# Issuing two experts' down blocks without waiting for the first two row gathers (one-core decoder layer)

## What is computed

```python
h2 = rms_norm(x, norm2_g) * (1 + scale2) + shift2
# hier_moe(h2, ...): the best of 4 groups, the 2 best of its 8 experts per token,
# tokens sorted by expert, then for each block of rows of one expert e:
xb = h_pad[toks]
a = xb @ w_exp_gate[e]          # (1024 x 512)
u = xb @ w_exp_up[e]            # (1024 x 512)
y = ((silu(a) * u) @ w_exp_down[e]) * wts   # (512 x 1024)
x = x + gate2 * y
```

## Time and profile before

| | us |
|---|---|
| median of 3 runs | 1310.64 |
| lowest, highest | 1309.82, 1310.77 |
| the profiled execution | 1311.63 |
| its span, first to last instruction | 1309.8 |

### The profile page before, as it was taken

How to read it: one execution, slowest core, us unless ns; L and a number is a source line. 1 busy time by engine, 2 the same in 40 slices (tenths; PEclk the granted TensorE clock), 3 DMA queues, 4 the chain that set the end, 5 groups by cost and what they waited for, 6 DMA issues and landing times.

```text
span 1309.8 us, 20856 instructions
## 1 busy us (share of the span) xinstructions
PE 1184.5 (90%) x8041; PEld 745.9 (57%) x8041; DVE 497.2 (38%) x1075; ACT 235.0 (18%) x536; POOL 235.1 (18%) x295
## 2 busy tenths in 40 slices
PE   4999998999999999999999998999987788787896
PEld 2344443475767777688888456656544444444463
DVE  3398966521324243454554456322211111111112
ACT  4122235322323232211001222000000000000000
POOL 2432344201102023340000101111111111111001
PEclk9899999999999999999999997999999999999989
DMA  9997999982654635312624627999999999999994
GB/s 355 372 278 269 361 372 385 378 330 65 248 175 142 172 94 134 98 22 57 176 84 175 257 64 209 408 414 419 410 417 419 416 418 418 416 416 416 415 413 152
DMA packets 117961, 368.17 MB, mean 281 GB/s; under 512 B 12556, under 2 KB 58525, under 8 KB 98406
## 3 DMA queue, kind: packets, MB, share of 16 engines
q1 hardware_dynamic: 93072, 304.50, 59.9%
q0 software_dynamic: 21328, 55.24, 13.7%
q10 hardware_dynamic: 3462, 7.07, 1.7%
HBM read 354.61 MB, written 22.36 MB: 288 GB/s over the span
## 4 chain that ended last, share of the span: by engine, by line
PE 63%; DMA 24%; SPq 7%; DVE 3%; issue 2%; ACT 1%; ACTq 0%; DVEq 0%; POOLq 0%
PE ps L1911 60%; DMA hx<-in_w_exp_gate 6%; DMA ring<-in_w_exp_gate 6%; SPq L549 4%; DMA ring<-in_w_exp_up 3%; DMA hx<-in_w_exp_up 3%; DMA ring<-in_w_in 3%; PE ps L1922 3%; SPq L554 2%; DMA ring<-in_cache_v 1%; DMA h_rows<-ring 1%; DVE work L1531 1%; DVE work L1866 0%; DMA work<-h_rows,idx 0%; DVE work L1641 0%
## 5 line engine op out<-in xcount | busy, mean ns | idle before, releaser
L1911 PE MATMUL ps<-ring,work 128*64 128x256 f32 (+4 forms) x2064 | 295.2, 437 | 42.1 <-DMA ring<-in_w_exp_up 17.5
L1911 PE MATMUL ps<-ring,hx 128*32 128x256 f32 (+3 forms) x1552 | 272.4, 444 | 7.4 <-ACT hx L834 4.2
L1911 PEld LDWEIGHTS ps<-ring,work 128*64 128x64 f32 (+2 forms) x2064 | 156.4, 139 | 162.8 <-issue 84.0
L1911 PEld LDWEIGHTS ps<-ring,hx 128*32 128x32 f32 (+1 forms) x1552 | 158.2, 147 | 104.1 <-issue 80.7
L1911 PE MATMUL ps<-hx,ring 128*128 128x272 f32 x704 | 163.8, 393 | 0.6 <-DVE work L1531 0.6
L1911 PE MATMUL ps<-work 128*32 128x256 f32 (+12 forms) x1186 | 135.8, 400 | 21.6 <-DVE work L1223 9.8
L1911 PEld LDWEIGHTS ps<-hx,ring 128*128 128x128 f32 x704 | 133.0, 190 | 28.7 <-DVE work L1531 1.1
L1911 PE MATMUL ps<-hx,work 128*64 128x256 f32 (+2 forms) x784 | 114.4, 414 | 22.6 <-DMA hx<-in_w_exp_up 11.4
L755 POOL DMA_INDIRECT out<-work x32 | 50.5, 1579 | 329.6 <-DVE work L1876 329.6
L1864 DVE TENSOR_TENSOR work<-work,ps 128x256 f32<-128x256 f32 x32 | 13.5, 421 | 250.6 <-ACT work L1171 250.6
L1911 PEld LDWEIGHTS ps<-hx,work 128*64 128x64 f32 (+2 forms) x784 | 66.9, 144 | 70.3 <-issue 26.4
(11 more groups left out here) (337 smaller groups left out, 949.2 us busy)
## 6 DMA issues: line engine op xcount, KB each, us to landing
ring<-in_w_exp_down SPq DMA_DIRECT2D x44, 1024.0 KB, 39.1
ring<-in_w_exp_gate SPq DMA_DIRECT2D x21, 2048.0 KB, 41.5
ring<-in_w_exp_up SPq DMA_DIRECT2D x21, 2048.0 KB, 40.9
ring<-in_w_ada SPq DMA_DIRECT2D x12, 2048.0 KB, 21.9
hx<-in_w_exp_up SPq DMA_DIRECT2D x11, 2048.0 KB, 40.7
hx<-in_w_exp_gate SPq DMA_DIRECT2D x11, 2048.0 KB, 41.6
work<-in_w_exp_down SPq DMA_DIRECT2D x20, 1024.0 KB, 39.7
ring<-in_cache_v SPq DMA_DIRECT2D x64, 256.0 KB, 10.0
```

The lines of the kernel that those rows point to most:

```text
L1911: return pe.matmul(out, lhsT, rhs, start=start, stop=stop, **k)
```

## The change

Two waits are taken out of SyncE's stream. The down blocks of experts 1 and 2 are then issued when the last logits are done and the last normed rows are stored.

```diff
             sp.wait_ge(s("lg_ps"), 5)
             sp.wait_ge(s("h2_out0"), 16 * 3)
             sp.wait_ge(s("h2_out1"), 16 * 2)
-            for p in range(2):
-                sp.wait_ge(s(f"xs_in{p}"), 16)
             down_load(1, expert_row(1))
             sp.wait_ge(s("x1_out"), 16 * PT)
             down_load(2, expert_row(2))
```

## The result

| | before | after |
|---|---|---|
| median of 5 runs, us | 1310.64 | 1316.95 |
| lowest, highest | 1309.73, 1310.98 | 1315.04, 1318.7 |
| the profiled execution | 1311.63 | 1316.95 |
| its span | 1309.8 | 1315.2 |

The ratio is 1.0048 with a 95% interval of 1.0037 to 1.0060: slower by 6.3 us. The forecast was 1311.4 us, no difference, with a range up to 1314.5. The sum leaned to the slow side by 0.8 us, the text called that no difference, and a rival had the slower outcome; none had the size.

What follows compares the result with a forecast made beforehand. DMA engines were taken to set the end. A gain of 4.2 us less a gather delay of 5.0 gave −0.8 us: 1312.4 us from the profiled execution, 1311.4 against the median, range 1307.9 to 1314.5.

Steps and rivals of the forecast that it cites:

- The sum: DMA time up to expert 3's gate load: gain of 4.2 us less d, −0.8 us with d = 5.0.
- the residual rows' wait: Wait of expert 2's down half: rows landed at 807.95 us, before the last store, so it costs nothing.
- credit: Gain from issuing the four down halves 7.5 us sooner, if the first gather is not delayed: 4.2 us.
- d: Delay of the first gather and so of TensorE's whole expert stage: 5.0 us, between 0 and 8.2.
- Rival 1: First gather hardly delayed, VectorE having slowed the third: d 1 or less, gain 3.2 to 4.2 us; chance 0.12.
- rival 3: Another wait, such as the residual rows, keeps the down halves' issue in place: 1310.6 us; chance 0.02.
- Rival 2: First gather meets a full queue: d 6.8 to 8.2, gate perhaps at the lower clock, about 1314 us; chance 0.26.
- the forecast's own band: Delay of the first gather between 1.6 and 6.8 us, with nearly no difference in time; chance 0.60.
- the sign of 821.6: First gather landing after 821.6 us would show that it met a full queue (Rival 2).
- ±1.7 us: Allowance for expert 0's gate at TensorE's lower or full clock: at most 1.7 us more, 1.8 less; costed at nothing.
- the third gather: Gather issued at 818.07 us beside the down blocks, landing after 8.2 us; taken as the first gather's nearest row.
- The rule of round robin alone: DMA engines alternate between queues by packet, so sharing alone delays the first gather: d = 3.4, gain 0.8 us.

Runs made afterwards that it cites:

- run 4: The changed kernel with VectorE idle from the index until the first gather has landed; 1314.86 us, ratio 1.0032.
- Run 2: The changed kernel, but only expert 1's two down halves go out early, expert 2's wait for both gathers; 1314.79 us, ratio 1.0038.
- run 1: The kernel before, but the down halves wait for the first gather only, not the second; 1310.98 us, ratio 1.0001.
- run 6: The changed kernel with 14, 6 or 8 extra matmuls of constants in TensorE's wait ahead of the first gather; 1317.69, 1312.96 and 1312.42 us.

## Why the prediction was wrong

**Right.** The DMA engines set the end; the halves go out at 810.4 (predicted 810.5); the residual rows' wait costs nothing; the first gather is what is delayed; the engines run dry between 824 and 832 us, and dip again before 845 (predicted near 840); the sum has the form "a credit less TensorE's lateness". With the measured x of 8.2 in place of d it gives −4.0 us, and by the bytes 4.4 were lost. Rival 1 was refuted by run 4, rival 3 by the first row of SyncE's issues. Rival 2 comes nearest, by its slower outcome and its slow gate, but not by its d: that was 6.5 and 6.2 us in the two profiles, inside the forecast's own band of 1.6 to 6.8, and the landing at 821.3 us stays under the sign of 821.6. Its 1314 us were too low. The ±1.7 us that the text kept for the clock never went into its range: 1314.5 is d near 8 alone.

**The step that failed: TensorE's lateness, taken as d = 5.0 us for the gather and nothing for the clock.** It was 8.2 us (x), and 6.8 in the second profile.

*The delay d.* Taken as 5.0 us from the third gather (8.2 us to landing), it was 6.5 and 6.2: 10.1 and 9.8 us to landing, 9.3 to 11.1 in the other runs beside 4 MB. The nearer row was the median of the later gathers, 10.3 us, which the text set aside for rival 2, because no long backlog stood ahead of the gather. Run 2 shows that 2 MB in flight are enough. The text also split the third gather's delay wrongly, into 3.4 us of sharing and 1.3 of a later start: q0's first packet came 4.6 us after that issue, where the first gather's came after 1.9, so that the later start is 2.7 us. In the changed kernel it is 3.3. The rule of round robin alone (Trainium skill, DMA: Bandwidth & Descriptors, Queues, rings and completion order), which gave 3.4 us, is further off still: it says how the queues share, and not when a gather's first packet comes or when the last engine is through.

*"Clock ... I cost it at nothing".* The row that prices it was there: a gate of 5.2 us with an up of 3.45 behind it, and the text's own bound of 1.7 us. In the profile the gate took 6.7 us, 1.5 more than before; in the second one 5.6, 0.3 more. That is no simple consequence of the longer wait, which grew from 1.9 to 9.5 us: behind a wait of 9.3 us the gate took 5.1 (run 4), and behind one of 2.4 us 6.6 (run 1). What decides when the clock comes back within the gate is not shown. The same gate takes 3.7 us when matmuls fill the wait (run 6).

**The sum.** 0.8 us were predicted and 5.6 came (y): 1.5 more by the gather, 1.5 by the gate, 0.2 by a later landing of the store, 0.4 by which the bytes lost exceed the formula, and 1.2 that no byte count shows. Over the runs with an x over 1 the credit, x less y, is 2.0 to 4.3 and not a firm 4.2. The formula treats the 16 engines as one. TensorE waits for the last of them at each load, and that the credit differs between runs fits this, but was not isolated. The medians are 6.3 and 7.1 us slower, more than these profiles show: the profile before stands 1.0 us above its median, and the second profile of the changed kernel 2.7 below its own.

## What to carry to other kernels

A transfer that is issued early into idle DMA engines was worth nothing here, because a small gather on the path had to share the engines with it: price the gather from its loaded landings, not from an idle or half-idle one. A delay ahead of TensorE's first matmuls of a stage can be paid twice, once as time and once as clock: the gate behind it took 6.7 us in one profile and 5.1 to 6.0 in four others, where 5.2 was the time before. So put what the stage takes at the lower clock into the range. Where the DMA engines set the end, ask after each move what they will do next; here they finished sooner and then waited for TensorE.

## What the runs showed of the hardware

- A gather of some 0.26 MB took 3.5 us with no down block beside it, 6.2 us beside 1 MB and 9.3 to 11.1 us beside 2 or 4 MB of plain loads, although 2.1 MB need only 4.9 us of the engines at 427 GB/s. Its queue's first packet came 1.9 us after the issue in the first case, 3.6 beside 1 MB, 4.7 beside 2 MB and 3.9 to 5.2 beside 4 MB. In the 2 MB case the last two us were spent on a few packets.
- TensorE's clock stayed at 0.50 (1.2 GHz) through 4.5 us of 128x16 matmuls back to back before the wait, and came back to 1.00 (2.4 GHz) within the 9.5 us of 128x512 matmuls that took the place of the wait in run 6 (mean 0.75). The same gate of 32 matmuls took 6.7 us, 5.2 or 3.7 by where that fell. The first row is the changed kernel's, the second run 6's:

```profile
807.40:811.90 4.50, 4.50 (x48) 4.37 (x48) 0.76 (x6) 1.69 (x3) 0.67 (x1) 0.50 0.59 132
811.86:821.37 9.51, 9.51 (x19) 4.37 (x19) 8.51 (x38) 0.00 (x0) 1.05 (x1) 0.75 1.00 376
```
- The chip's stage ahead of the experts ended up to 2.9 us sooner in one profile than in another, which is why times within the expert stage are counted from its last store here.
